# First block's output projections: order of updates, low parts and sums of squares around the norms, and the place of two weight loads in the queue

## The chip, the cores and the metric

The kernel runs on 1 core of one Trainium2 chip. The metric is the device time of one execution in microseconds (us). TensorE is called PE here, VectorE DVE, ScalarE ACT, and SyncE SP; SP issues the loads. Lines such as L901 are lines of the kernel before.

## What is computed

Two transformer blocks of two layers each run one after the other, on one sequence of 256 tokens with width 1024 (the first block adds 16 meta tokens, so it has 272 columns; its second layer drops them again at the output projection). Every layer of the first block ends its mixer with a projection `w_out` that is added to the residual, and then runs a gated feed-forward network (FFN) on the normed residual:

```
def rms_norm(x, g):
    xf = x.astype(jnp.float32)
    y = xf * lax.rsqrt(jnp.mean(xf * xf, axis=-1, keepdims=True) + EPS)
    return (y * g.astype(jnp.float32)).astype(x.dtype)
```

The second block is modulated by vectors `c @ w_ada + b_ada`. They depend on no token, so the kernel computes them in small pieces ("slots", 48 of them) scattered over the first block and the second.

## The kernel before, in words

The residual `H_t` lies transposed, eight tiles of 128 features by 272 (or 256) tokens. A product in float32 is made of three faster ones: an operand is split into a high part (rounded, by ACT) and a low part (the rest, by DVE), and PE adds high by high, high by low and low by high (line L901; 24 matmuls per output tile for 8 tiles of features).

Weights come in chunks of 1 MB into `raw`, a ring of RAW = 4 buffers. SP issues the loads in one fixed order (`load`, L782, for weights, and `ada_load`, L769, for slots), and each waits until the buffer's former chunk is done with: `sp.wait_ge(raw_done[...])`. A weight chunk is done when the low parts of both its halves are made (`split_lo`, L1535, from `raw` and the high part that `split_hi`, L2255, wrote); a slot chunk is done when PE has used it (`ada_sums`, L842).

The high and low parts go to `WH_t` and `WL_t`, four places each. `Linear.freed` tells which later half chunk may be split once an output tile is finished; with `w_out`, whose rest has four output tiles (k = 4 to 7), those are the two halves of the first two chunks of the next weights, `w_gu`.

`w_out` is two `Linear` objects: `first` (k = 0 to 3) and `rest` (k = 4 to 7). For each output tile PE writes a bank of `PA`; DVE adds it to the residual (L1597); ACT squares the new residual tile (`square`, L2291); DVE adds the square to the running sum `acc` (`accumulate`, L1546). The three engines each work through one queue in order, and this order is written out by hand in `linear_dve` and `linear_act`:

```
elif L.stat and k >= (KD - 3 if L.kt == KD else KD - 1):
    accumulate(L.stat, k)
    deferred.extend(todo[q])
elif L.stat:
    splits(q)
    accumulate(L.stat, k)
```

So for k = 0 to 4 of `w_out` DVE makes the freed low part between the residual's update and the accumulation, and for k = 5, 6 and 7 it puts the low part off (`deferred`) until after the norm's reciprocal. ACT makes the high part ahead of its wait for the residual's update, for all k but 7.

Then the norm (class `Norm`; `norm_pe`, `norm_dve`, `norm_act`). PE multiplies `acc` by ones, four matmuls of a quarter of the tokens each, which gives the sums over features in four groups of partitions (L1043; the trace shows each as two passes); ACT takes the root (L2491), DVE the reciprocal (L1701), PE spreads it over all partitions (L1056), ACT copies it to `rt` (L2501), and DVE scales the residual with it (L1716), tile by tile; ACT rounds the high part (L2513) and DVE makes the low part (L1724). The first linear after it, `w_gu`, goes over the tiles as they come: `four_tiles` computes four output tiles at a time, first with the weights' high parts (L961), last with the low parts (L989).

A norm can have slots of the modulation to fill PE's waits (`Norm.fill`, `norm_slots_pe`). In the two FFN norms of the first block there is one slot ahead of the sums ("start") and one behind the spreading ("end"). Their chunks are loaded ahead of all chunks of `w_gu`, because `tail_ada = AdaSlots(2)` stands ahead of the FFN in the plan.

There are six norms of this kind: the first (on the input), the two FFN norms of the first block, its second mixing norm, the norm that starts the second block, and the last one, behind the last FFN. The four others of the second block are of another class, `Joint`.

## Time and profile before

| what | value |
|---|---|
| median of 3 runs | 1711.11 us (1710.5 to 1714.62) |
| the profiled execution's own time | 1713.17 us |
| its span | 1711.2 us |
| PE busy | 1619.1 us, 95% of the span |
| DVE busy, ACT busy | 1020.6 us (60%), 869.0 us (51%) |
| mean granted TensorE clock | 0.979 |
| DMA | 253.92 MB, 148 GB/s |

A timeline row has the start, the duration, the engine, the line, the operation with output and inputs, how many in a row, and in brackets how long the engine stood idle before it and what it waited for. Durations of PE are of pipelined matmuls, so that starts overlap ends. The granted clock is 1.00 at 2.4 GHz and 0.50 at 1.2 GHz.

### The profile page before, as it was taken

To read this page: it belongs to the slowest core of one execution; us is meant where nothing else is said; L and a number is where in the kernel's file an instruction comes from. 1 tells how busy PE (TensorE), PEld (TensorE's weight loads), DVE (VectorE), ACT (ScalarE), POOL (GpSimd) and SP (SyncE) were. 2 spreads that over 40 slices of the span, in tenths; PEclk is the share of its full clock that TensorE was granted. 3 is DMA by queue.
4 is the path that set the end of the run, shared out by engine and by line. 5 is a ranking of instruction groups with operands and counts; after the bars stand their busy time and mean duration, and the time that the engine had idled before them with its cause. 6 is when DMAs were issued, how large, how long until landed. Compare 5 with 4: busy or idle time off the path is not lost.

```text
span 1711.2 us, 27924 instructions
## 1 busy us (share of the span) xinstructions
PE 1619.1 (95%) x11722; PEld 1419.0 (83%) x11722; DVE 1020.6 (60%) x1586; ACT 869.0 (51%) x1467; POOL 21.0 (1%) x38
## 2 busy tenths in 40 slices
PE   6998999989998999999989999999999898999997
PEld 6967999989778999887757778888888674789997
DVE  7665545465846555733464765425556777687676
ACT  6754434447545444535365544323444547666563
POOL 0000000000000000130000000000000000000000
PEclk9998999999998999999999999999999899999999
DMA  7364546354555464682201453232213530154642
GB/s 294 145 239 162 187 144 211 130 192 151 204 197 197 144 229 144 209 236 74 91 9 50 150 220 118 75 138 101 83 57 119 197 123 26 70 211 153 220 145 90
DMA packets 60523, 253.92 MB, mean 148 GB/s; under 512 B 4976, under 2 KB 8304, under 8 KB 42480
## 3 DMA queue, kind: packets, MB, share of 16 engines
q1 hardware_dynamic: 59088, 249.01, 40.0%
q0 software_dynamic: 1312, 3.15, 1.0%
q8 instruction: 93, 1.52, 0.3%
q14 instruction: 30, 0.25, 0.0%
HBM read 251.09 MB, written 1.05 MB: 147 GB/s over the span
## 4 chain that ended last, share of the span: by engine, by line
PE 62%; DVE 4%; ACT 3%; issue 1%; DVEq 0%; ACTq 0%
PE PA L901 49%; PE PA L961 3%; PE PB L1305 2%; PE PA L989 1%; PE PB L842 1%; PE PB L1292 1%; DVE WL_t L1535 1%; ACT tmp L2694 1%; PE PA L1377 1%; PE PA L937 1%; PE PA L938 1%; PE PA L943 1%; PE PA L1489 1%; PE PA L1383 0%; DVE small L2117 0%
## 5 line engine op out<-in xcount | busy, mean ns | idle before, releaser
L1535 DVE TENSOR_TENSOR WL_t<-raw,WH_t 128x1024 fp32r<-128x1024 f32 (+1 forms) x344 | 444.4, 1297 | 325.7 <-ACT WH_t L2255 325.4
L901 PE MATMUL PA<-XH_t,WH_t 128*128 128x256 f32 (+2 forms) x1984 | 630.2, 318 | 4.9 <-DVE XL_t L1724 2.3
L901 PE MATMUL PA<-XL_t,WH_t 128*128 128x256 f32 (+2 forms) x1984 | 624.8, 315 | 0.0
L901 PE MATMUL PA<-XH_t,WL_t 128*128 128x256 f32 (+2 forms) x1984 | 624.7, 315 | 0.0
L2255 ACT ACTIVATE WH_t<-raw 128x1024 fp32r<-128x1024 f32 (+1 forms) x344 | 380.9, 1112 | 172.1 <-PE PA L901 143.2
L901 PEld LDWEIGHTS PA<-XH_t,WH_t 128*128 128x128 f32 x1984 | 377.2, 190 | 34.7 <-issue 7.9
L901 PEld LDWEIGHTS PA<-XL_t,WH_t 128*128 128x128 f32 x1984 | 377.3, 190 | 21.3 <-issue 0.5
L901 PEld LDWEIGHTS PA<-XH_t,WL_t 128*128 128x128 f32 x1984 | 377.2, 190 | 21.2
L901 PE MATMUL PA<-AH_t,WH_t 128*128 128x256 f32 (+2 forms) x616 | 192.2, 312 | 0.3 <-DVE AL_t L1581 0.2
L901 PE MATMUL PA<-AH_t,WL_t 128*128 128x256 f32 (+2 forms) x616 | 191.1, 310 | 0.0
L901 PE MATMUL PA<-AL_t,WH_t 128*128 128x256 f32 (+2 forms) x616 | 190.5, 309 | 0.0
L1651 DVE SCALAR_TENSOR_TENSOR tmp<-PA,par,tmp 128x510 f32<-128x510 f32 (+1 forms) x88 | 53.7, 614 | 121.8 <-ACT tmp L2409 121.8
L2409 ACT ACTIVATE tmp<-PA,par 128x512 f32<-128x512 f32 (+1 forms) x88 | 58.4, 667 | 133.7 <-PE PA L901 126.0
L901 PEld LDWEIGHTS PA<-AH_t,WL_t 128*128 128x128 f32 x616 | 115.8, 188 | 6.8
L901 PEld LDWEIGHTS PA<-AH_t,WH_t 128*128 128x128 f32 x616 | 115.8, 188 | 6.6 <-DVE AL_t L1581 0.9
L901 PEld LDWEIGHTS PA<-AL_t,WH_t 128*128 128x128 f32 x616 | 115.7, 188 | 6.4
L2366 ACT ACTIVATE big<-PA 128x272 f32<-128x272 f32 (+2 forms) x68 | 31.6, 465 | 122.4 <-PE PA L901 109.8
L961 PE MATMUL PA<-XH_t,WH_t 128*128 128x256 f32 (+1 forms) x288 | 52.4, 318 | 5.4 <-DVE XL_t L1724 2.7
L842 PE MATMUL PB<-raw,cpad_t 128*32 128x256 f32 x768 | 57.2, 422 | 0.0
L961 PEld LDWEIGHTS PA<-XH_t,WH_t 128*128 128x128 f32 x288 | 44.6, 218 | 13.9 <-issue 9.4
L2694 ACT ACTIVATE tmp<-PA,small 128x512 f32<-128x512 f32 (+1 forms) x64 | 40.2, 638 | 26.2 <-DVE small L2117 26.2
L2117 DVE TENSOR_REDUCE small<-PA 128x1 f32<-128x512 f32 (+1 forms) x64 | 36.8, 618 | 27.1 <-PE PA L1489 13.2
(277 smaller groups left out, 1705.2 us busy)
## 6 DMA issues: line engine op xcount, KB each, us to landing
raw<-in_w_ada SPq DMA_DIRECT2D x48, 1024.0 KB, 4.9
raw<-in_w_gu SPq DMA_DIRECT2D x44, 1024.0 KB, 4.8
raw<-in_w_dn SPq DMA_DIRECT2D x64, 704.0 KB, 4.0
raw<-in_w_up SPq DMA_DIRECT2D x44, 1024.0 KB, 4.8
raw<-in_w_in SPq DMA_DIRECT2D x30, 1024.0 KB, 4.9
raw<-in_w_out SPq DMA_DIRECT2D x12, 1024.0 KB, 4.8
raw<-in_w_qkv SPq DMA_DIRECT2D x6, 1024.0 KB, 6.6
raw<-in_w_outc SPq DMA_DIRECT2D x4, 1024.0 KB, 4.8
```

What stands on the lines that cost most here:

```text
L842: mm = pe.matmul(ada_psum[b // 6][0][32 * j:32 * j + 32, :], cpad[:, k, :], RAWV[:, r % RAW, c:c + 256], start=(k == 0), stop=(k == 7))
L901: mm = pe.matmul(PA[:, (L.b0 + o) % 4, 0:T], W[:, c:c + P], X[:, k, L.x0:L.x0 + T], start=(n == 0 and m == 0 and not L.early), stop=(n == ...
L937: pe.matmul(PA[:, bank, 0:L.T], WH_t[:, c:c + P], hi[:, k, 0:L.T], start=(k == 0), stop=False)
L961: pe.matmul(PA[:, bank % 4, a:b], WH_t[:, c:c + P], x[:, k, a:b], start=(k == 0 and x is hi), stop=False)
L1305: mm = pe.matmul(PB[64 * c:64 * c + 64, v % 2, 0:256], value(v, c, kb), a_PT(second, v % 2)[c][:, j, :], start=(j == 0), stop=(j == len(bl ...
L1535: dve.tensor_tensor(WL_t[:, w:w + L.cols], RAWV[:, r % RAW, part * UNIT:part * UNIT + L.cols], WHf[:, w:w + L.cols], ALU.subtract).then_in ...
L1651: dve.scalar_tensor_tensor(c[:, :, 1:SEQ], ps[:, :, 0:SEQ - 1], tap(o, 0), c[:, :, 1:SEQ], ALU.mult, ALU.add).then_inc(S("conv_left"), 1)
L2117: dve.tensor_reduce(a_m[p % 3][:, c:c + 1], PA[:, 2 * (p % 2) + c, 0:width(p)], AX_X, ALU.max, negate=True).then_inc(S(name + "_m"), 1)
L2255: act.activation(WH_t[:, w:w + L.cols], RAWV[:, r % RAW, part * UNIT:part * UNIT + L.cols], ACT.Copy).then_inc(S("w_hi"), 1)
L2366: act.activation(L.dst[:, k, 0:T], PA[:, (L.b0 + o) % 4, 0:T], ACT.Copy).then_inc(S("of_act"), 1)
L2409: act.activation(conv[s % 2][x][:, 0:T], PA[:, (L.b0 + o) % 4, 0:T], ACT.Identity, bias=biasv(L.layer)[:, bass.ds(c, 1)], scale=tapv(L.lay ...
L2694: act.activation(a_P[p % 3][c][:, 0:w], PA[:, 2 * (p % 2) + c, 0:w], ACT.Exp, bias=a_m[p % 3][:, c:c + 1], accum_out=a_s[p % 3][:, c:c + 1 ...
```

## The change

- `Norm` gets a number `own`: 3 for a norm behind `w_out` (kt == KD), 1 for a norm behind an FFN, 0 for the first. The squares of the last `own` tiles are written to places of their own in `tmp` (`own_squares`), DVE does not accumulate them, and PE adds them itself: four matmuls for `acc`, then four for each own square, in one accumulation.
- Behind `w_out`, DVE accumulates the square of tile k - 1 after the update of tile k, and makes the low part that tile k - 1 freed after that; only the last low part is put off past the reciprocal. ACT waits for the update and squares first, and makes the freed high part after that.
- In the two FFN norms the slot "start" becomes a slot "amid", between the sums and the spreading. Both slots' chunks are now loaded behind the first two chunks of `w_gu` (`held=2`).

```diff
-            def __init__(self, kind, l, T, src, groups, alone=False):
+            def __init__(self, kind, l, T, src, groups, alone=False, own=0):
...
-                self.a0 = take("n_acc", KD - 1)
+
+                self.own = own
+                self.a0 = take("n_acc", KD - 1 - own)
...
-            n = Norm(*a, alone=not writers)
+            n = Norm(*a, alone=not writers, own=0 if not writers else 3 if writers[-1].kt == KD else 1)
...
-            tail_ada = AdaSlots(2)
             n = norm([first, rest], "pre", l, T, HV, [(0, T, ("ffng", l), None)])
-            n.fill(tail_ada.slots(), start=1, end=1)
-            writers = [ffn(l, T, "glu", w_gu1, w_dn1, HV, tiles_ready(n), mods=(0, 0, 6) if l else None)[1]]
+
+
+            up, last = ffn(l, T, "glu", w_gu1, w_dn1, HV, tiles_ready(n), held=2, mods=(0, 0, 6) if l else None)
+            n.fill(up.slots(), amid=1, end=1)
+            writers = [last]
...
+        def own_squares(n, k):
+
+
+            return tmp[:, 1536 + (KD - 1 - k) * 512:1536 + (KD - 1 - k) * 512 + n.T]
...
-                pe.wait_ge(S("n_acc"), n.value("n_acc", KD - 1))
+                pe.wait_ge(S("n_acc"), n.value("n_acc", KD - 1 - n.own))
...
-                for j in range(4):
-                    x = acc[:, j * w:(j + 1) * w] if n.T < T2 else quarter(acc, j)
-                    o = PB[32 * j:32 * j + 32, 0, 0:w]
-                    mm = pe.matmul(o if n.T < T2 else o.rearrange("p (h t) -> p h t", h=2), ones[:, 0:32], x,
-                                   start=True, stop=True)
+                for k in range(KD - 1 - n.own, KD):
+                    x = acc if k == KD - 1 - n.own else own_squares(n, k)
+                    if x is not acc:
+
+                        pe.wait_ge(S("n_sq"), n.value("n_sq", k))
+                    for j in range(4):
+                        q = x[:, j * w:(j + 1) * w] if n.T < T2 else quarter(x, j)
+                        o = PB[32 * j:32 * j + 32, 0, 0:w]
+                        mm = pe.matmul(o if n.T < T2 else o.rearrange("p (h t) -> p h t", h=2), ones[:, 0:32], q,
+                                       start=x is acc, stop=k == KD - 1)
                 mm.then_inc(S("n_sum"), 1)
+                norm_slots_pe(n, "amid")
...
-                if k == 0:
+                if k == 0 or k >= KD - n.own:
                     return
...
-                            elif L.stat and k >= (KD - 3 if L.kt == KD else KD - 1):
-                                accumulate(L.stat, k)
-                                deferred.extend(todo[q])
-                            elif L.stat:
+                            elif L.stat and L.kt == FH and k < KD - 1:
                                 splits(q)
                                 accumulate(L.stat, k)
+                            elif L.stat:
+
+                                if L.kt == KD:
+                                    accumulate(L.stat, max(k - 1, 0))
+                                for x in late:
+                                    split_lo(*x)
+                                late[:] = todo[q]
+                                if k == KD - 1:
+                                    deferred.extend(late)
+                                    late.clear()
...
+                elif k >= KD - n.own:
+                    dst = own_squares(n, k)
...
-                                last = k == KD - 1
-                                if not last:
+                                ahead = L.kt == FH and k < KD - 1
+                                if ahead:
                                     splits(q)
...
-                                if last:
+                                if k == KD - 1:
                                     deferred.extend(todo[q])
+                                elif not ahead:
+                                    splits(q)
```

How the rows move is shown at the first FFN norm (first layer of the first block). Each row has the line, the operation and how often it stands in a row.

DVE before, from the update of tile k = 4 on. `H_t<-H_t,PA` is an update, `WL_t<-raw,WH_t` a low part of weights, `tmp<-tmp` an accumulation:

```order
L1597 TENSOR_TENSOR H_t<-H_t,PA 128x272
L1535 TENSOR_TENSOR WL_t<-raw,WH_t 128x1024
L1546 TENSOR_TENSOR tmp<-tmp 128x272
L1597 TENSOR_TENSOR H_t<-H_t,PA 128x272
L1546 TENSOR_TENSOR tmp<-tmp 128x272
L1597 TENSOR_TENSOR H_t<-H_t,PA 128x272
L1546 TENSOR_TENSOR tmp<-tmp 128x272
L1597 TENSOR_TENSOR H_t<-H_t,PA 128x272
L1546 TENSOR_TENSOR tmp<-tmp 128x272
L1701 RECIPROCAL tmp<-tmp 128x68
L1535 TENSOR_TENSOR WL_t<-raw,WH_t 128x1024
```
DVE in the change, from the update of tile k = 4 on:

```order
L1612 TENSOR_TENSOR H_t<-H_t,PA 128x272
L1561 TENSOR_TENSOR tmp<-tmp 128x272
L1550 TENSOR_TENSOR WL_t<-raw,WH_t 128x1024
L1612 TENSOR_TENSOR H_t<-H_t,PA 128x272
L1561 TENSOR_TENSOR tmp<-tmp 128x272
L1550 TENSOR_TENSOR WL_t<-raw,WH_t 128x1024
L1612 TENSOR_TENSOR H_t<-H_t,PA 128x272
L1550 TENSOR_TENSOR WL_t<-raw,WH_t 128x1024
L1612 TENSOR_TENSOR H_t<-H_t,PA 128x272
L1550 TENSOR_TENSOR WL_t<-raw,WH_t 128x1024
L1723 RECIPROCAL tmp<-tmp 128x68
L1550 TENSOR_TENSOR WL_t<-raw,WH_t 128x1024
```
No low part stands between an update and the accumulation of its own tile any longer, three accumulations are gone, and two low parts more stand ahead of the reciprocal, each behind a later tile's update; one stands behind it, as before.

PE before: the last matmuls of `w_out`, a slot, the sums, the spreading, a slot, the first of `w_gu`:

```order
L901 MATMUL PA<-XL_t,WH_t 128x272
L901 MATMUL PA<-XH_t,WL_t 128x272
L842 MATMUL PB<-raw,cpad_t 32x256 x8
L1043 MATMUL PB<-tmp,cboth 32x68 x4
L1056 MATMUL PA<-tmp,spread 128x68 x4
L842 MATMUL PB<-raw,cpad_t 32x256 x8
L961 MATMUL PA<-XH_t,WH_t 128x272 x4
```
PE in the change, the same place:

```order
L910 MATMUL PA<-XL_t,WH_t 128x272
L910 MATMUL PA<-XH_t,WL_t 128x272
L1057 MATMUL PB<-tmp,cboth 32x68 x16
L851 MATMUL PB<-raw,cpad_t 32x256 x8
L1071 MATMUL PA<-tmp,spread 128x68 x4
L851 MATMUL PB<-raw,cpad_t 32x256 x8
L970 MATMUL PA<-XH_t,WH_t 128x272 x4
```
The sums grow from 4 to 16 matmuls and stand directly behind `w_out`; the slot that stood ahead of them stands behind them.

SP before, the loads from `w_out`'s first half on:

```order
L782 DMA raw<-in_w_out 128x2048 x2
L769 DMA raw<-in_w_ada 128x4x512 x8
L782 DMA raw<-in_w_out 128x2048 x2
L769 DMA raw<-in_w_ada 128x4x512 x4
L782 DMA raw<-in_w_gu 128x2048 x11
L782 DMA raw<-in_w_dn 128x1408 x8
```
SP in the change:

```order
L791 DMA raw<-in_w_out 128x2048 x2
L778 DMA raw<-in_w_ada 128x4x512 x8
L791 DMA raw<-in_w_out 128x2048 x2
L778 DMA raw<-in_w_ada 128x4x512 x2
L791 DMA raw<-in_w_gu 128x2048 x2
L778 DMA raw<-in_w_ada 128x4x512 x2
L791 DMA raw<-in_w_gu 128x2048 x9
```
Two chunks of `w_gu` have moved ahead of the last two slots' chunks (the first two of the four after `w_out` belong to the mixer and stay).

## Rows read from the trace of the kernel before

**Rows 1.** The page, part 4: the chain that ended last, by engine.

```profile
PE 62%; DVE 4%; ACT 3%; issue 1%; DVEq 0%; ACTq 0%
```

**Rows 2.** DVE timeline, first FFN norm (start us, us, engine line op, [idle before <-releaser]).

```profile
148.91 0.43 DVE L1597 TENSOR_TENSOR H_t<-H_t,PA 128x272 f32<-128x272 f32 x1
157.23 1.23 DVE L1535 TENSOR_TENSOR WL_t<-raw,WH_t 128x1024 fp32r<-128x1024 f32 x1 [7.89 <-ACT WH_t L2255]
...
161.29 0.43 DVE L1597 TENSOR_TENSOR H_t<-H_t,PA 128x272 f32<-128x272 f32 x1
162.27 0.44 DVE L1546 TENSOR_TENSOR tmp<-tmp 128x272 f32<-128x272 f32 x1 [0.55 <-ACT tmp L2291]
163.64 0.58 DVE L1701 RECIPROCAL tmp<-tmp 128x68 f32<-128x68 f32 x1 [0.93 <-ACT tmp L2491]
...
165.48 0.92 DVE L1716 SCALAR_TENSOR_TENSOR tmp<-H_t,par,tmp 128x272 f32<-128x272 f32 x2 [0.19 <-ACT tmp L2501]
```

**Rows 3.** ACT timeline, the same stretch.

```profile
156.14 1.06 ACT L2255 ACTIVATE WH_t<-raw 128x1024 fp32r<-128x1024 f32 x1 [8.16 <-DMA raw<-in_w_gu]
...
161.81 0.43 ACT L2291 ACTIVATE tmp<-H_t 128x272 f32<-128x272 f32 x1 [0.90 <-DVE H_t L1597]
163.29 0.32 ACT L2491 ACTIVATE tmp<-PB,small 128x68 f32<-128x68 f32 x1 [1.05 <-PE PB L1043]
```

**Rows 4.** PE timeline, the same stretch.

```profile
157.37 0.29 PE L901 MATMUL PA<-XH_t,WL_t 128*128 128x272 f32 x1
157.59 1.07 PE L842 MATMUL PB<-raw,cpad_t 128*32 128x256 f32 x16
162.76 0.45 PE L1043 MATMUL PB<-tmp,cboth 128*32 128x68 f32 x8 [4.11 <-DVE tmp L1546]
...
164.27 0.71 PE L1056 MATMUL PA<-tmp,spread 32*128 32x68 f32 x8 [1.05 <-DVE tmp L1701]
...
167.17 1.25 PE L961 MATMUL PA<-XH_t,WH_t 128*128 128x272 f32 x4 [0.33 <-DVE XL_t L1724]
...
171.63 0.67 PE L961 MATMUL PA<-XL_t,WH_t 128*128 128x272 f32 x4
```

**Rows 5.** SP queue: two issues; then two DMA issues, KB, us to landing.

```profile
145.00 0.37 SPq L769 DMA_DIRECT2D raw<-in_w_ada  x1
...
148.67 0.37 SPq L769 DMA_DIRECT2D raw<-in_w_ada  x1
...
raw<-in_w_ada SPq DMA_DIRECT2D x1, 1024.0 KB, 4.9
...
raw<-in_w_gu SPq DMA_DIRECT2D x1, 1024.0 KB, 7.0
```

**Rows 6.** Second FFN norm: ACT timeline, then PE timeline.

```profile
511.35 1.06 ACT L2255 ACTIVATE WH_t<-raw 128x1024 fp32r<-128x1024 f32 x1 [8.53 <-DMA raw<-in_w_gu]
...
518.35 0.31 ACT L2491 ACTIVATE tmp<-PB,small 128x64 f32<-128x64 f32 x1 [1.02 <-PE PB L1043]
...
517.83 0.44 PE L1043 MATMUL PB<-tmp,cboth 128*32 128x64 f32 x8 [5.21 <-DVE tmp L1546]
```

**Rows 7.** Stretches, line L961 alone: window, PE busy, PEld busy, granted clock.

```profile
167.10:177.20 10.10, 10.03 (x64) 10.00 (x64) 0.79 0.72 272
522.10:531.90 9.80, 9.75 (x64) 9.57 (x64) 0.78 0.74 288
```

**Rows 8.** Stretches of 1 us on PE at the first FFN norm.

```profile
161.00:162.00 1.00, 0.00 (x0) 0.55 0.98 418
```

**Rows 9.** Second mixing norm: PE timeline, then its clock in 1 us.

```profile
371.63 0.33 PE L1043 MATMUL PB<-tmp,cboth 128*32 128x68 f32 x8 [1.51 <-DVE tmp L1546]
...
372.00:373.00 1.00, 0.00 (x0) 0.87 0.06 12
```

**Rows 10.** DVE timeline: last accumulation before second block, and at the end.

```profile
714.99 0.69 DVE L1546 TENSOR_TENSOR tmp<-tmp 128x512 f32<-128x512 f32 x1 [0.74 <-ACT tmp L2291]
...
1699.81 0.42 DVE L1546 TENSOR_TENSOR tmp<-tmp 128x256 f32<-128x256 f32 x1 [0.53 <-ACT tmp L2291]
```

More of the change, by code:

```diff
@@ L1569, in tail_product @@
                                   ALU.mult).then_inc(S("j_b"), 1)
-            deferred = []
+            deferred, late = [], []
             def linear_dve(L):
```

## The prediction

> **What bounds the kernel now.** I read the page's chain first: PE carries 62% of what ended last, and DVE and ACT come in short pieces [rows 1]. Time is to be had only where PE waits. So I went to the norms that the diff touches and read, for each, the timelines of PE, DVE and ACT, then the loads, then the granted clock.
>
> At the first FFN norm PE ends `w_out` at 157.66 (157.37 + 0.29), does the "start" slot, and then stands idle for 4.11 us until the last accumulation [rows 4]. DVE shows why. The update of tile 4 starts at 148.91; the low part queued behind it waits 7.89 us for ACT's high part, and the updates of tiles 5 to 7, whose matmuls PE had done long before or by then, come only after it, the last at 161.29 [rows 2]. ACT's high part waited 8.16 us for the load of the first chunk of `w_gu` [rows 3]. That load is late because it stands behind two slot chunks in SP's queue: the second slot's load was issued at 148.67, the first `w_gu` chunk came right behind it and took 7.0 us to land, where a load with nothing ahead takes 4.9 [rows 5]. The second FFN norm repeats it: a wait of 8.53 us for `w_gu`, and PE idle for 5.21 us [rows 6]. So a load that nobody needs for another 10 us holds up, through two in-order queues, a sum that everybody waits for.
>
> The idle time has a second price. The granted clock stays at 1.00 while PE is busy and falls inside the idle gap (0.55 on average in the microsecond from 161) [rows 8]. The first 64 matmuls of `w_gu` (L961) then run at a mean clock of 0.79 and 0.78 and take 10.03 and 9.75 us [rows 7]; a group of four takes 1.25 us in the slow part (some 0.91 from start to start) and 0.67 (0.51 from start to start) once the clock is back [rows 4].
>
> **The change, part by part.** DVE's updates of tiles 5 to 7 stand ahead of their low parts, and ACT's squares ahead of its high parts. Behind `w_out`'s end at 157.66 the path is then: update at 157.70; square 0.52 later, as 161.29 and 161.81 are apart, at 158.22 [rows 2, 3]; where the accumulation stood (0.46 after the square's start) PE now starts the last four sums itself, at about 158.7; with 0.33 us for a sum at full clock [rows 9] the root starts at 159.1 instead of 163.29 [rows 3]: **4.2 us less**. At the second FFN norm `w_out` ends at 511.6 (the sums start at 517.83 after 5.21 idle, and the slot ahead took 1.0) and the same 1.4 us give a root at 513.05 instead of 518.35 [rows 6]: **5.3 us less**.
>
> This needs the loads to keep up. DVE makes each low part of `w_out` one tile later, which moves the buffer releases: the first `w_gu` load goes out some 1.1 us after the place at which the first slot load went (145.00), at 146.1 [rows 5], and the second some 1.9 us after 148.67, behind an update and an accumulation, at about 150.6. With 4.9 us they land by 151.5 and 155.5. ACT has to have made the third high part (1.06 us [rows 3]) before 158.2, so the second chunk may land at 157.1: 1.6 us to spare, at the second FFN norm about 0.9. The low parts of `w_out`'s own tiles stay ahead of PE by about 1.5 us. Both are cover that I cost at nothing; a load later than that costs one for one.
>
> The sums: 12 matmuls more behind `w_out`, 24 passes. Eight passes take at most 0.33 us at full clock [rows 9], so 24 take at most 1.0; `acc` and squares 5 and 6 are ready at 157.66, and PE has 1.05 us before the last square. Nothing. Three accumulations less on DVE (0.44 each [rows 2]) count above only through the last.
>
> The slot "amid" takes 1.07 us at full clock, and 1.05 us pass between sums and spreading [rows 4]. It fits, if its chunk has landed: behind the second `w_gu` chunk, about 158.0 (155.5 plus 2.5: the first `w_gu` chunk landed at 156.1 and the slot ahead of it at 153.6 [rows 5]), needed at 158.9. At the second norm that is 512.7 against 512.8, and I take 0.3 us for waits there. Bounds: nothing to 1 us at each. SP's queue holds the same loads; only the order of the four changes, at 0.37 us an issue.
>
> Behind the reciprocal DVE makes the one deferred low part. Its high part is made only after the root now, where before it was long there: the root's 0.32, 1.06 for the high and 1.23 for the low part put the scaling up to 0.4 us later in the chain than 165.48 has it [rows 2, 3]. Taken: 0.24 at each, 0.5 together.
>
> The clock. PE's longest gap at these norms shrinks from 4.11 and 5.21 us to about 1.3 us, and two slots of 1.0 us stand in it. If the clock stays up, L961 takes 16 groups of 0.51 us and 0.48 us, with 0.2 of waits for the first tiles 8.3 and 7.9 us instead of 10.03 and 9.75: **3.6 us less** for both. The rows at the second mixing norm warn: there PE's longest gap was only 1.51 us, and the clock fell all the same (0.87 in the microsecond from 372) [rows 9]. But there PE did next to nothing else in some 6 us, while here two slots come. I take the clock as staying up.
> The Trainium skill ("TensorE: Matmul & The Clock Gate", "Why this matters for your kernels") asks only that there be no long idle gaps between bursts of matmuls; by that rule the clock would stay up here, and also at the second mixing norm, where the trace disagrees with it.
>
> Three norms behind an FFN lose only the last accumulation from the path: 0.44 at the second mixing norm (as rows 2), 0.69 at the start of the second block and 0.42 at the end [rows 10]. The first two are followed by a stretch at the lower clock whose end need not move with them. Taken: 0.4, 0.6 and 0.5 with the hand-over, **1.5 us**.
>
> Sum: 4.2 + 5.3 + 3.6 + 1.5 - 0.5 - 0.3 = 13.8 us. The profiled execution's span of 1711.2 becomes 1697.4, and its own time of 1713.17 becomes 1699.4; that execution was 2 us above the median of 1711.11, so the median becomes **1697.3**. Behind `w_gu`'s start PE is the engine that is waited for, so nothing later should eat the gain.
>
> **Rivals.**
> 1. The clock falls anyway, in the new, shorter gap. For it: the second mixing norm [rows 9]. Against: two slots of real matmuls in the gap. Then 3.6 us are not won, and the slot "amid" may run at half speed and hold the spreading by 0.9 at one norm: 9.3 to 10.2 us, about 1701. Chance 0.22.
> 2. The loads are late by a few microseconds: `w_gu`'s second chunk lands after 157.1 (the longest landing here, 7.0 us, would be 157.6), or the slot's chunk lands late and PE, in order, holds the spreading for it. 1.5 to 4 us at each norm, and the clock with them: a gain of 5 to 8 us, about 1704. Chance 0.12.
> 3. The new order is slower, through the slot "amid". Before, no slot stood between the sums and the spreading; now PE stops there for a chunk that is queued behind two others, and the spreading, the scaling and all of `w_gu` are queued behind it. Each microsecond of landing past 158.9 costs one. To eat 13.8 us at two norms the chunk must be 7 us late at each, that is land 15 us after its issue at about 151. The rows have 4.9 alone and 7.0 second in the queue, and I reckon with 7. Chance 0.02, time 1713 to 1718.
> 4. The change does less than it says: something else (the copies, the weights' low parts) sets the start of `w_gu`, and only the accumulations are won, 0.5 us at each of five norms. Against: both waits end in `w_gu`'s landing. 1708 to 1709. Chance 0.04.
>
> **How the numbers follow.** My forecast has 0.60. Its own range is 13.8 plus or minus 2 (the slots' waits up to 1.7 us more, the clock's edges at the other norms, which move by up to a microsecond each way), 1695 to 1699.5. The range that should hold the time 8 times in 10 goes up over rival 1 and part of rival 2: 1694.5 to 1703.5. About 0.3%, or 5.1 us, is what a measurement can tell from no change, so faster means below 1706: the forecast, rival 1, nearly all of rival 2 and some of rival 4, 0.93; the same 0.05; slower 0.02.
>
> **What would show it.** In the profile after, at the first FFN norm: DVE's updates of tiles 5 to 7 start 0.04 us behind PE's tiles, with no wait of 8 us anywhere on DVE; ACT waits for `w_gu` once, for 2 us or so, behind the square of tile 4; the sums show 32 passes, the last eight some 1.0 us after `w_out`'s end; the spreading starts 1.0 us behind the root; L961 starts about 5.4 us after `w_out`'s end (before 9.5) and takes 8.3 us at clock 1.00. I am wrong if DVE or ACT still stands for a load ahead of the square of tile 7, if PE waits for a slot's load ahead of the spreading, or if the clock falls before L961.

## The result and the profile after

The change takes 1702.45 us (median of 6 runs, 1701.05 to 1707.42), the kernel before on the same chip 1711.25 (6 runs, 1710.38 to 1718.37). The ratio is 0.9947, with a 95% interval of 0.9933 to 0.996: 8.8 us less, in the range, where 13.8 were forecast. The profiled execution of after is the slowest of its six: own time 1707.42, span 1705.6. So its total says little; its stretches say much.

Read first what the page's chain says, and how far back it reaches. The shares of after sum to the whole span. Those of before [rows 1] sum to 70%: its chain is followed back from the end only to 516.03 us, and its first FFN norm is not on it. So 62% and 83% for PE can't be compared. What the chain of after does show is that one load of `w_ada`, the slots' weights, is on it: it starts at 501.81 and takes 10.70 us, at the second FFN norm.

```profile
PE 83%; DVE 9%; ACT 6%; issue 2%; DMA 1%; SPq 0%; DVEq 0%; ACTq 0%
```

**First FFN norm.** DVE's timeline of after (start us, us, engine line op, [idle before <-releaser]; L1612 is the update, L1550 the low part, L1723 the reciprocal, L1738 the scaling), to hold against [rows 2]:

```profile
155.74 0.44 DVE L1612 TENSOR_TENSOR H_t<-H_t,PA 128x272 f32<-128x272 f32 x1 [1.08 <-PE PA L910]
156.09 1.22 DVE L1550 TENSOR_TENSOR WL_t<-raw,WH_t 128x1024 fp32r<-128x1024 f32 x1
158.75 0.44 DVE L1612 TENSOR_TENSOR H_t<-H_t,PA 128x272 f32<-128x272 f32 x1 [1.44 <-PE PA L910]
...
160.51 0.58 DVE L1723 RECIPROCAL tmp<-tmp 128x68 f32<-128x68 f32 x1 [0.18 <-ACT tmp L2517]
161.46 1.23 DVE L1550 TENSOR_TENSOR WL_t<-raw,WH_t 128x1024 fp32r<-128x1024 f32 x1 [0.37 <-ACT WH_t L2277]
162.60 0.91 DVE L1738 SCALAR_TENSOR_TENSOR tmp<-H_t,par,tmp 128x272 f32<-128x272 f32 x2
```

ACT's timeline, to hold against [rows 3] (L2277 high part, L2315 square, L2517 root):

```profile
152.10 1.06 ACT L2277 ACTIVATE WH_t<-raw 128x1024 fp32r<-128x1024 f32 x1 [1.42 <-DMA raw<-in_w_gu]
...
159.28 0.43 ACT L2315 ACTIVATE tmp<-H_t 128x272 f32<-128x272 f32 x1 [1.63 <-DVE H_t L1612]
160.16 0.32 ACT L2517 ACTIVATE tmp<-PB,small 128x68 f32<-128x68 f32 x1 [0.45 <-PE PB L1057]
```

And PE's timeline, to hold against [rows 4] (L910 the products of `w_out`, L1057 the sums, L851 a slot, L1071 the spreading, L970 and L998 those of `w_gu` with its high and its low parts):

```profile
158.43 0.29 PE L910 MATMUL PA<-XH_t,WL_t 128*128 128x272 f32 x1
158.65 0.56 PE L1057 MATMUL PB<-tmp,cboth 128*32 128x68 f32 x24
159.77 0.33 PE L1057 MATMUL PB<-tmp,cboth 128*32 128x68 f32 x8 [0.56 <-ACT tmp L2315]
159.91 1.05 PE L851 MATMUL PB<-raw,cpad_t 128*32 128x256 f32 x16
161.14 0.45 PE L1071 MATMUL PA<-tmp,spread 32*128 32x68 f32 x8 [0.19 <-DVE tmp L1723]
162.02 1.07 PE L851 MATMUL PB<-raw,cpad_t 128*32 128x256 f32 x16 [0.42 <-DMA raw<-in_w_ada]
164.28 0.74 PE L970 MATMUL PA<-XH_t,WH_t 128*128 128x272 f32 x4 [1.20 <-DVE XL_t L1746]
...
172.40 0.79 PE L998 MATMUL PA<-XH_t,WL_t 128*128 128x272 f32 x5
```

The wait of 7.89 us on DVE is gone, ACT waits 1.42 us for `w_gu`, and PE's 4.11 us have shrunk to 0.56 for the last square. `w_out` ends at 158.72 (158.43 + 0.29); the root follows 1.44 us behind (160.16), where before it took 5.63. L970 starts 5.56 us behind `w_out`'s end and takes 8.12 us to L998's start, at full clock. (L998's row counts 5 because the stretch shown ends there.) So the first product with a low part of `w_gu` (L998) stands 13.68 us behind `w_out`'s end; before it stood 19.55 behind. I use this distance as the measure of a norm from here on, since it holds the waits and the clock together: **5.9 us won** at this norm.

**Second FFN norm.** PE's timeline of after, to hold against [rows 6]:

```profile
507.44 0.32 PE L1057 MATMUL PB<-tmp,cboth 128*32 128x64 f32 x8 [0.55 <-ACT tmp L2315]
509.87 1.26 PE L851 MATMUL PB<-raw,cpad_t 128*32 128x256 f32 x16 [2.12 <-DMA raw<-in_w_ada]
511.07 0.70 PE L1071 MATMUL PA<-tmp,spread 32*128 32x64 f32 x8
512.55 1.93 PE L851 MATMUL PB<-raw,cpad_t 128*32 128x256 f32 x16 [0.79 <-DMA raw<-in_w_ada]
514.42 1.22 PE L970 MATMUL PA<-XH_t,WH_t 128*128 128x256 f32 x4
...
523.51 0.76 PE L998 MATMUL PA<-XH_t,WL_t 128*128 128x256 f32 x5
```

`w_out` ends at 506.41 and the root is again 1.41 us behind it. Then PE stands 2.12 us for the chunk of the slot "amid", with the spreading queued behind. The chunk's load went out 6.14 us ahead of `w_out`'s end and took 9.6 us. The chunk of the slot "end" is late too: PE stands 0.79 us more for it, the slot takes 1.93 us, and L970 follows it with no idle time. This is the load that the chain names. Issues of DMA of after, in the stretch 500.2 to 500.4 (KB, us to landing):

```profile
raw<-in_w_ada SPq DMA_DIRECT2D x1, 1024.0 KB, 9.6
```

Then the clock falls. Stretches of 1 us of after (window, length, busy time of PE, PEld, DVE, ACT, POOL, then granted clock, DMA share, GB/s); the first is the first FFN norm, where before had 0.55 [rows 8]:

```profile
161.00:162.00 1.00, 0.45 (x8) 0.31 (x8) 0.63 (x2) 0.76 (x2) 0.00 (x0) 1.00 1.11 444
...
510.00:511.00 1.00, 1.00 (x16) 0.29 (x12) 0.34 (x1) 0.00 (x0) 0.00 (x0) 0.81 0.97 403
511.00:512.00 1.00, 0.77 (x12) 0.52 (x8) 0.00 (x0) 0.16 (x1) 0.00 (x0) 0.50 1.07 436
```

The stretches of L970 alone (PE busy, PEld busy, clock), to hold against [rows 7]:

```profile
164.10:172.60 8.50, 8.28 (x64) 8.08 (x64) 1.00 0.88 359
514.30:523.60 9.30, 9.18 (x64) 9.05 (x64) 0.83 0.64 250
```

The low parts start 17.10 us behind `w_out`'s end, before 20.11: **3.0 us won** where I had 6.9.

**The other norms.** At the second mixing norm the root is 1.44 us behind the end of the products, before 1.91; at the start of the second block 1.81, before 2.52. The clock falls at the mixing norm as before [rows 9], and at the start of the second block in both. Not all of the 0.71 us is kept there: the first product with a low part comes 15.84 us behind the end of the products in after and 17.07 in a second trace of the same kernel (k8_after_again below), before 16.71. Over the nine traces in which PE adds the last square at this norm the mean is 16.40, over the four without 16.97.

**What this execution lost elsewhere.** Two losses don't belong to the norms. It reached `w_out`'s end at the first FFN norm 1.06 us later than before did, though nearly all of the program up to there is the same; the 192 matmuls of `w_out` take 31.59 us with no idle time, before 31.60, so the loss lies ahead of them. And in the attention of the second block PE stands while ACT makes exponentials, and the clock falls there, in a stretch that had 1.00 in the trace of before (1400 to 1420). PE's timeline, then 1 us of clock of after:

```profile
1409.21 2.08 PE L1504 MATMUL PA<-big 64*128 64x512 f32 x4 [2.75 <-ACT tmp L2720]
```

```profile
1408.00:1409.00 1.00, 0.00 (x0) 0.00 (x0) 0.22 (x1) 1.00 (x5) 0.00 (x0) 0.66 1.04 391
```

### The profile page after: what moved, and what is told of

It reads as the page before. It is cut to its first block, busy times and chain, and to the rows that moved or that the text cites. A ratio compares the mean times of both kernels' runs of the same rounds, so it can differ in the third digit from the quotient of the medians.

```text
span 1705.6 us, 28040 instructions
## 1 busy us (share of the span) xinstructions
PE 1619.8 (95%) x11794; PEld 1418.1 (83%) x11794; DVE 1017.1 (60%) x1577; ACT 869.4 (51%) x1467; POOL 21.1 (1%) x38
## 4 chain that ended last, share of the span: by engine, by line
PE 83%; DVE 9%; ACT 6%; issue 2%; DMA 1%; SPq 0%; DVEq 0%; ACTq 0%
PE PA L910 63%; PE PA L970 4%; DVE WL_t L1550 2%; PE PB L851 2%; PE PB L1320 2%; PE PA L998 2%; PE PB L1307 1%; ACT WH_t L2277 1%; PE PA L946 1%; PE PA L947 1%; PE PA L952 1%; PE PA L865 1%; PE PA L1504 1%; PE PB L1250 1%; DMA raw<-in_w_ada 1%
## 5 line engine op out<-in xcount | busy, mean ns | idle before, releaser
L910 PE MATMUL PA<-XH_t,WH_t 128*128 128x256 f32 (+2 forms) x1984 | 629.6, 317 | 4.9 <-DVE XL_t L1746 2.4
L1550 DVE TENSOR_TENSOR WL_t<-raw,WH_t 128x1024 fp32r<-128x1024 f32 (+1 forms) x344 | 444.5, 1297 | 312.0 <-ACT WH_t L2277 311.6
L910 PE MATMUL PA<-XL_t,WH_t 128*128 128x256 f32 (+2 forms) x1984 | 624.1, 315 | 0.0
L910 PE MATMUL PA<-XH_t,WL_t 128*128 128x256 f32 (+2 forms) x1984 | 623.8, 314 | 0.0
L2277 ACT ACTIVATE WH_t<-raw 128x1024 fp32r<-128x1024 f32 (+1 forms) x344 | 380.8, 1111 | 155.2 <-PE PA L910 139.7
L910 PEld LDWEIGHTS PA<-XH_t,WH_t 128*128 128x128 f32 x1984 | 376.8, 190 | 34.5 <-issue 7.9
L910 PEld LDWEIGHTS PA<-XH_t,WL_t 128*128 128x128 f32 x1984 | 376.9, 190 | 21.6
L910 PEld LDWEIGHTS PA<-XL_t,WH_t 128*128 128x128 f32 x1984 | 377.2, 190 | 21.2 <-issue 0.5
L910 PE MATMUL PA<-AH_t,WH_t 128*128 128x256 f32 (+2 forms) x616 | 192.0, 312 | 0.3 <-DVE AL_t L1596 0.2
L910 PE MATMUL PA<-AH_t,WL_t 128*128 128x256 f32 (+2 forms) x616 | 190.9, 310 | 0.0
L910 PE MATMUL PA<-AL_t,WH_t 128*128 128x256 f32 (+2 forms) x616 | 190.3, 309 | 0.0
L910 PEld LDWEIGHTS PA<-AH_t,WL_t 128*128 128x128 f32 x616 | 115.6, 188 | 6.8
L910 PEld LDWEIGHTS PA<-AH_t,WH_t 128*128 128x128 f32 x616 | 115.6, 188 | 6.6 <-DVE AL_t L1596 0.9
L910 PEld LDWEIGHTS PA<-AL_t,WH_t 128*128 128x128 f32 x616 | 115.6, 188 | 6.5
L2390 ACT ACTIVATE big<-PA 128x272 f32<-128x272 f32 (+2 forms) x68 | 31.6, 465 | 123.2 <-PE PA L910 110.1
L851 PE MATMUL PB<-raw,cpad_t 128*32 128x256 f32 x768 | 55.6, 413 | 3.3 <-DMA raw<-in_w_ada 3.3
L970 PE MATMUL PA<-XH_t,WH_t 128*128 128x256 f32 (+1 forms) x288 | 50.0, 306 | 7.4 <-DVE XL_t L1746 3.5
L970 PEld LDWEIGHTS PA<-XH_t,WH_t 128*128 128x128 f32 x288 | 42.2, 206 | 14.7 <-issue 10.0
```

The source lines that it names most:

```text
L851: mm = pe.matmul(ada_psum[b // 6][0][32 * j:32 * j + 32, :], cpad[:, k, :], RAWV[:, r % RAW, c:c + 256], start=(k == 0), stop=(k == 7))
L910: mm = pe.matmul(PA[:, (L.b0 + o) % 4, 0:T], W[:, c:c + P], X[:, k, L.x0:L.x0 + T], start=(n == 0 and m == 0 and not L.early), stop=(n == ...
L970: pe.matmul(PA[:, bank % 4, a:b], WH_t[:, c:c + P], x[:, k, a:b], start=(k == 0 and x is hi), stop=False)
L1550: dve.tensor_tensor(WL_t[:, w:w + L.cols], RAWV[:, r % RAW, part * UNIT:part * UNIT + L.cols], WHf[:, w:w + L.cols], ALU.subtract).then_in ...
L2277: act.activation(WH_t[:, w:w + L.cols], RAWV[:, r % RAW, part * UNIT:part * UNIT + L.cols], ACT.Copy).then_inc(S("w_hi"), 1)
L2390: act.activation(L.dst[:, k, 0:T], PA[:, (L.b0 + o) % 4, 0:T], ACT.Copy).then_inc(S("of_act"), 1)
```

## The experiments

What they had to decide. The theory of the **loads**: the gain is all in their place (third part of the change: no slot chunk ahead of `w_gu`), and the new order on DVE and ACT makes the slot's chunk late, because it moves the release of the buffers. Its rival, the **order**: the updates and squares ahead of the splits are what frees the sum. And for the loss at the second norm a rival of its own: it is the **clock** that fell there by itself, and not the late chunk. Below, "1st" and "2nd" are the distance from `w_out`'s end to the first product with a low part of `w_gu`, in the profiled execution; before has 19.55 and 20.11, the change 13.68 and 17.10.

**k1_old_slots: the change with the loads in their old place.**

```diff
+            tail_ada = AdaSlots(2)
             n = norm([first, rest], "pre", l, T, HV, [(0, T, ("ffng", l), None)])
-            up, last = ffn(..., held=2, ...)
-            n.fill(up.slots(), amid=1, end=1)
+            n.fill(tail_ada.slots(), start=1, end=1)
+            writers = [ffn(...)[1]]
```

> The change without its third part: updates ahead of low and high parts and own squares as in the change, but both slots' chunks are loaded ahead of w_gu again, and the slots stand at start and end. Theory (the place of the loads is what frees the sum): w_gu's first chunk lands some 0.3 us before w_out's end or later, at both FFN norms ACT stands for it with the squares of tiles 5 to 7 queued behind, the root comes at most 1 us earlier than before, and the gain is that of the three norms behind an FFN, 1.5 us, plus 0.5: about 1709.5. Rival (the order of updates and low parts is what frees it): as the whole change, about 1702.5.

Measured: 1714.02 us (12 runs), before 1713.11 (18 runs): ratio 1.0013 (1.0001 to 1.0024). 1st 19.79, 2nd 20.64. The new order and the three squares alone win nothing at the FFN norms, as ACT's timeline at the first one shows:

```profile
159.24 1.06 ACT L2275 ACTIVATE WH_t<-raw 128x1024 fp32r<-128x1024 f32 x1 [8.33 <-DMA raw<-in_w_gu]
160.20 0.41 ACT L2313 ACTIVATE tmp<-H_t 128x272 f32<-128x272 f32 x1
```

The same 8 us as [rows 3], one tile later: a square is now ahead of the high part of its own tile, but still behind that of the tile before. The first chunk of `w_gu` lands 0.28 and 1.69 us behind `w_out`'s end, where before it landed 1.60 and 0.35 ahead of it. The order moves a wait and takes none away. The time missed its forecast of 1709.5: the roots at the three other norms came 0.4 to 0.7 us earlier, and yet the kernel is no faster than before. The section on the prediction comes back to this.

**k2_slots_alone and k11_slots_again: before with the third part alone.** The old order on DVE and ACT, and all eight accumulations on DVE.

```diff
                 mm.then_inc(S("n_sum"), 1)
+                norm_slots_pe(n, "amid")
...
-            n.fill(tail_ada.slots(), start=1, end=1)
+            up, last = ffn(..., held=2, ...)
+            n.fill(up.slots(), amid=1, end=1)
```

> The kernel before with the third part of the change alone: slots amid and end, their chunks behind the first two of w_gu; the order on DVE and ACT and the sums are those of before. Theory: w_gu's first chunk goes out at the place of the first slot's load and lands 6 us before w_out's end, so updates and squares no longer wait; the root comes 0.45 us later than in the change (the last accumulation is on the path), but the loads go out 1 to 2 us earlier than in the change, so that PE does not wait for the slot amid at the second FFN norm and the clock stays up there: 12 us less than before, about 1699, at least as fast as the whole change. Rival (all three parts are needed): 1704 to 1708, with DVE's low parts still ahead of updates.

> k2_slots_alone again. Theory: as the change or 1 us below it, 9 to 10 us below the kernel before; PE never waits for the slot amid.

Measured: 1702.93 (5 runs), before 1713.11, ratio 0.995 (0.9936 to 0.9964); again, on another chip, 1704.01 (6 runs), before 1711.7, ratio 0.995 (0.9935 to 0.9964). This one part has the ratio of the whole change; the 1699 that I expected at first was too low. 1st 13.64, 2nd 13.14 (again 13.64 and 13.15). PE's timeline at the first FFN norm of k2_slots_alone, and the last sums and the slots of the second:

```profile
157.53 0.33 PE L1045 MATMUL PB<-tmp,cboth 128*32 128x68 f32 x8 [1.52 <-DVE tmp L1549]
157.68 1.05 PE L844 MATMUL PB<-raw,cpad_t 128*32 128x256 f32 x16
...
505.12 0.32 PE L1045 MATMUL PB<-tmp,cboth 128*32 128x64 f32 x8 [1.47 <-DVE tmp L1549]
505.26 1.05 PE L844 MATMUL PB<-raw,cpad_t 128*32 128x256 f32 x16
...
506.84 1.07 PE L844 MATMUL PB<-raw,cpad_t 128*32 128x256 f32 x16
```

No slot waits at either norm. The slot "amid" has its chunk 0.52 us ahead of `w_out`'s end at the second. Only the accumulation is left, 1.52 and 1.47 us of idle PE, and the clock stays up over it. The theory of the order falls, that of the loads stands.

**k3_early_low: the change, but tiles 0 to 3 of `w_out` in the old order.**

```diff
-                            elif L.stat and L.kt == FH and k < KD - 1:
+                            elif L.stat and k < (KD - 1 if L.kt == FH else KD // 2):
```

(and the same bound for ACT's squares and for the accumulation one tile back)

> The change, but for tiles 0 to 3 of w_out DVE and ACT make the freed parts as early as in the kernel before; the new order holds from tile 4 on. Theory (what is missing from the forecast is PE's wait of 2.1 us for the slot amid at the second FFN norm, and the clock that falls in it): the second w_gu chunk and both slots' chunks go out some 1.5 us earlier, PE's wait for the slot at the second FFN norm shrinks below 0.6 us, the clock stays at 1.00 there, and the time is 2.5 to 3.5 us below the change, about 1699.5. Rival (what is missing is the clock's phase in the second block's attention, which differs from execution to execution): as the change, 1702.5.

Measured: 1701.24 (5 runs), ratio 0.9936 (0.9922 to 0.9951). 1st 15.25, 2nd 13.23. The time lies between what theory and rival gave, and its interval overlaps the change's. At the second norm the slot's load goes out 7.71 us ahead of `w_out`'s end, not 6.14, and the slot "amid" doesn't wait. At the first norm nothing on PE waits for a load, and the clock falls all the same. PE's timeline there (the second row is cut off by the end of its stretch), then stretches of 1 us:

```profile
156.98 1.07 PE L851 MATMUL PB<-raw,cpad_t 128*32 128x256 f32 x16
159.74 0.57 PE L970 MATMUL PA<-XH_t,WH_t 128*128 128x272 f32 x2 [1.69 <-DVE XL_t L1746]
```

```profile
159.00:160.00 1.00, 0.26 (x2) 0.29 (x3) 0.96 (x3) 0.49 (x3) 0.00 (x0) 1.00 0.97 197
160.00:161.00 1.00, 1.00 (x6) 1.00 (x6) 1.00 (x4) 0.78 (x2) 0.00 (x0) 0.50 0.86 344
```

1.6 us at this norm are the clock's alone (15.25 against 13.68). So rival 1 of the prediction is real without any late load.

**k4_no_own1: the change, but squares summed by PE only behind `w_out`.** (`own=3` there, 0 at the norms behind an FFN.)

> The change without own squares behind an FFN (own = 3 behind w_out, 0 elsewhere). Theory: the last accumulation is on the path at three norms again, 0.44, 0.69 and 0.42 us, so the time is 1.0 to 1.5 us above the change, about 1704. Rival (the clock's edges do not move with the work, so the two norms followed by a stretch at the lower clock give nothing): 0.5 us above the change.

Measured: 1706.58 (7 runs), ratio 0.9962 (0.9947 to 0.9978). The roots of the other norms are back at 1.91 and 2.52 us. By the traces that is 1.6 us over the three norms (0.47, 0.71 and 0.46); the difference from the ratio of the change, 0.9962 to 0.9945 (k8_after_again), would be 2.9, with intervals that overlap. 1st 13.67, 2nd 16.58, and again PE waits for the slot "amid":

```profile
511.80 1.07 PE L851 MATMUL PB<-raw,cpad_t 128*32 128x256 f32 x16 [1.14 <-DMA raw<-in_w_ada]
```

**k8_after_again: the change once more, on another chip.**

> The change again, on the chip of the next three, to compare them with. Theory: at the second FFN norm PE again waits 1 to 2.5 us for the slot amid, since its chunk lands 1 us or more behind the sums, and w_gu's low parts start 16.5 to 17.5 us behind w_out's end (13.7 at the first norm). Rival (that wait was one execution's accident): below 14.5 us at both.

Measured: 1704.09 (5 runs), before 1713.37 (9 runs), ratio 0.9945 (0.993 to 0.9959). 1st 13.68, 2nd 14.55: 5.6 us won where the first trace had 3.0. The 14.55 is outside the 16.5 to 17.5 of the theory and just above the rival's bound of 14.5, so the size of the first trace's loss was in large part that one execution's. PE's timeline at the second FFN norm:

```profile
505.74 1.07 PE L851 MATMUL PB<-raw,cpad_t 128*32 128x256 f32 x16 [0.20 <-DMA raw<-in_w_ada]
506.74 0.45 PE L1071 MATMUL PA<-tmp,spread 32*128 32x64 f32 x8
508.43 1.79 PE L851 MATMUL PB<-raw,cpad_t 128*32 128x256 f32 x16 [1.24 <-DMA raw<-in_w_ada]
510.15 1.23 PE L970 MATMUL PA<-XH_t,WH_t 128*128 128x256 f32 x4
```

A wait of 0.20 us, then one of 1.24 that in part overlaps what DVE needs anyway, and the second slot at 1.79 us instead of 1.07, since the clock had fallen. The size of the loss differs from one execution to the next; its place doesn't.

**k5_end2 and k6_early_end2: no slot between sums and spreading.** k5 is the change with both slots behind the spreading, k6 is k3_early_low with the same.

```diff
-            n.fill(up.slots(), amid=1, end=1)
+            n.fill(up.slots(), end=2)
```

> The change with both slots behind the spreading. Theory: at the second FFN norm the spreading starts 2.4 us behind w_out's end instead of 3.5 to 4.6, but the second slot's chunk lands at +5 to +6 and PE does it ahead of w_gu, so w_gu starts at +6 to +7 instead of +7 to +8: 1 us less there. At the first norm both slots end at +4.4 to +5.3, ahead of w_gu's start at +5.57: nothing. The time is 1 to 2 us below the change. Rival (with no matmuls between the sums and the spreading the clock falls at both norms): 1 to 3 us above the change.

> Early low parts for tiles 0 to 3, and both slots behind the spreading. Theory: the chunks are there in time in either place, so it is as with the slot amid (w_gu starts 5.5 us behind w_out's end at both norms): the time of k3_early_low, 1.2 us below the change. Rival on the clock: the slot amid keeps it up; without it the clock falls, and the low parts of w_gu start 15 to 16 us behind w_out's end at both norms: 2 to 3 us above k3_early_low.

Measured: k5 1702.26 (5 runs), ratio 0.9931 (0.9918 to 0.9943), 1st 13.67, 2nd 13.23; k6 1701.86 (5 runs), ratio 0.9931 (0.9919 to 0.9944), 1st 13.67, 2nd 13.95. In k5 the chunk still lands 1.42 us behind `w_out`'s end, but nobody needs it before 2.74, so the second norm gets its full 6.9 us. In k6 no slot waits for its chunk at all, and yet the clock falls at the second norm and takes 0.7 us. PE's timeline there, then 1 us:

```profile
505.94 0.45 PE L1071 MATMUL PA<-tmp,spread 32*128 32x64 f32 x8 [1.02 <-DVE tmp L1723]
...
507.00:508.00 1.00, 1.00 (x16) 0.52 (x12) 1.00 (x3) 0.07 (x1) 0.00 (x0) 0.61 0.80 336
```

The interval of k5 overlaps that of the change (0.993 to 0.9959): the traces put it 1.3 us (k8) to 3.9 us (after) ahead at the second norm, and the timings alone don't decide.

**k7_slots_own1 and k10_own1_again: the parts that were worth it.** The third part, the old order on DVE and ACT, and one square summed by PE at all five norms.

```diff
-own=0 if not writers else 3 if writers[-1].kt == KD else 1
+own=1 if writers else 0
...
-                            elif L.stat and L.kt == FH and k < KD - 1:
-                                splits(q)
-                                accumulate(L.stat, k)
-                            elif L.stat:
-                                ...
+                            elif L.stat and k >= (KD - 3 if L.kt == KD else KD - 1):
+                                accumulate(L.stat, k)
+                                deferred.extend(todo[q])
+                            elif L.stat:
+                                splits(q)
+                                accumulate(L.stat, k)
...
-                                ahead = L.kt == FH and k < KD - 1
+                                ahead = k < KD - 1
```

> The slots' third part with the old order on DVE and ACT, and one own square at all five norms: it beats both kernels if the order of low parts is worth nothing. Theory: as the slots alone, less 0.45 us at each FFN norm and 1.0 to 1.5 us at the three others; 2 us below k2_slots_alone and 1.5 us below the change. Rival (updates ahead of low parts matter): as k2_slots_alone, above the change.

> k7_slots_own1 again, beside the slots alone on the same chip. Theory: 2.3 us (0.45 at five norms, 0.7 for one of them) below k11_slots_again, and w_gu's low parts start 13.3 and 12.7 us behind w_out's end. Rival (its lead over the change came from where the clock fell in those executions): no lead over the slots alone.

Measured: 1696.44 (5 runs), before 1713.37, ratio 0.991 (0.9894 to 0.9926); again, on another chip, 1697.79 (6 runs), before 1711.7, ratio 0.992 (0.9905 to 0.9935). This beats both kernels: the first interval lies wholly below the change's. But the lead over the slots alone (k2, k11) is 6.5 and 6.2 us in the medians, where 2 and 2.3 were expected and the traces give 0.4 to 0.5 us at each norm. The rest is not shown to be the square's. From the end of the products ahead of the second block to the end of the last products, k7 and k10 take 982.7 us, k2 and k11 989.3 and 988.2; the clock falls at about 1400 and 1452 us in k2 and k11 and not in k7 and k10, and the programs differ there by that one norm alone. 1st 13.25, 2nd 12.69 (again 13.17 and 12.69). PE's timeline of k10_own1_again, first and second FFN norm:

```profile
159.06 0.33 PE L1057 MATMUL PB<-tmp,cboth 128*32 128x68 f32 x8 [0.79 <-ACT tmp L2308]
159.20 1.05 PE L851 MATMUL PB<-raw,cpad_t 128*32 128x256 f32 x16
160.44 0.45 PE L1071 MATMUL PA<-tmp,spread 32*128 32x68 f32 x8 [0.19 <-DVE tmp L1716]
160.82 1.07 PE L851 MATMUL PB<-raw,cpad_t 128*32 128x256 f32 x16
163.08 0.74 PE L970 MATMUL PA<-XH_t,WH_t 128*128 128x272 f32 x4 [1.19 <-DVE XL_t L1739]
...
509.07 1.07 PE L851 MATMUL PB<-raw,cpad_t 128*32 128x256 f32 x16 [0.65 <-DMA raw<-in_w_ada]
510.56 0.71 PE L970 MATMUL PA<-XH_t,WH_t 128*128 128x256 f32 x4 [0.41 <-DVE XL_t L1739]
```

Here `w_gu` starts 5.07 us behind `w_out`'s end (4.94 at the second), not 5.57 (5.48 in k5). DVE's timeline at the second norm tells why: its one deferred low part follows the reciprocal with no wait, since ACT made the high part long ago. At the first norm of after it waited 0.37 for ACT and started 0.95 us behind the reciprocal's start, here 0.47.

```profile
507.37 0.55 DVE L1716 RECIPROCAL tmp<-tmp 128x64 f32<-128x64 f32 x1 [1.30 <-ACT tmp L2510]
507.84 1.16 DVE L1550 TENSOR_TENSOR WL_t<-raw,WH_t 128x1024 fp32r<-128x1024 f32 x1
508.92 0.87 DVE L1731 SCALAR_TENSOR_TENSOR tmp<-H_t,par,tmp 128x256 f32<-128x256 f32 x2
```

**k9_own3_old_order: the same with the change's three squares behind `w_out`.** That is, the change without its new order and nothing else.

> The whole change except its new order on DVE and ACT: slots amid and end behind two chunks of w_gu, three own squares behind w_out, one behind an FFN; low and high parts where they stood before. Theory: the accumulations of tiles 5 and 6 are hidden anyway, so three own squares are worth what one is, and the time is that of k7_slots_own1 within 0.5 us, 3 to 7 us below the change. Rival (the order is worth something once the squares are PE's): above k7_slots_own1.

Measured: 1700.41 (6 runs), before 1711.7, ratio 0.993 (0.9917 to 0.9944). 1st 13.17, 2nd 12.69, to the hundredth those of k10_own1_again: with three squares or with one, the last square is what is waited for. Its clock fell in the trace at places far from these norms where that of k10 did not (at 1406 and 1454 us), so the 2.6 us between the medians of k9 and k10 are not shown to be the squares', and the intervals overlap.

**The slot's load, over all traces.** At the second FFN norm, in us from `w_out`'s end; the slot "amid" needs the chunk at +1.2 (+1.6 where DVE makes the last accumulation, +2.7 in k5 and k6):

| Order on DVE and ACT | issued | took | landed |
|---|---|---|---|
| new (after, k4, k8, k5) | -6.14 | 9.55, 8.57, 7.64, 7.56 | +3.41, +2.43, +1.50, +1.42 |
| old, or old for tiles 0 to 3 (k2, k11, k7, k10, k9, k6, k3) | -7.71 | 7.19, 7.09, 7.34, 7.09, 8.50, 8.55, 8.68 | -0.52, -0.62, -0.36, -0.61, +0.79, +0.85, +0.97 |

From issue to need the new order leaves 7.3 us, and all four loads took longer; the old one leaves 8.9, and all seven took less. That is the late chunk of the slot "amid", and no clock is needed for it. The rival of the clock holds in part: k3 (first norm) and k6 (second) show it falling with no wait of PE for any load.

## Why the prediction was right and wrong

- **"PE carries 62% of what ended last."** Misread: the chain of [rows 1] covers 70% of the span, from 516.03 us on, so this is 62 of 70. Nothing in the sum rests on it.
- **The root, 4.2 and 5.3 us.** Right: 1.44 and 1.41 us behind `w_out`'s end, against 5.63 and 6.73 before, so 4.2 and 5.3. But I gave the whole to the order on DVE and ACT. k1 shows that the order wins none of it, and k2 that the place of the loads wins all but 0.4 to 0.5, the last accumulation. The row that I had quoted, `w_gu` landing in 7.0 us behind two slots [rows 5], held the whole cause; with the loads in time, the order of the queue behind them doesn't matter.
- **"This needs the loads to keep up."** The issues were right: 11.48 and 7.04 us ahead of `w_out`'s end for `w_gu`, forecast 11.56 and 7.06 (first norm).
- **The slot "amid", "0.3 us for waits there".** This is the step that failed. At the first norm no wait, and 2.7 us from the chunk of `w_gu` to the slot's, forecast 2.5. At the second norm I had reckoned the chunk at 512.7 against a need at 512.8, that is with no cover, and with the same 2.5; measured 4.93, 4.12 and 2.92, and waits of 2.12, 1.14 and 0.20 us. My upper bound of 1 us was too low: [rows 5] has one landing of each kind, and I took its scatter to be nothing. The first step to see was that the new order moves the issue 1.57 us back for no gain.
- **The clock, "I take the clock as staying up", 3.6 us.** Right at the first norm: 1.00 throughout, 8.1 us for the 64 matmuls. Wrong at the second, in after, k4 and k8: 9.1 us in after. 2.12 us of wait for the slot "amid" became 3.9 us of loss (17.10 against the 13.23 of k5): the chunk of the slot "end" was late as well, and from 510.6 us on the clock was at its lower level. Rival 1 named this, rival 2 the late slot's chunk; both came, at one norm.
  The rule of the Trainium skill that I had weighed ("TensorE: Matmul & The Clock Gate", "Why this matters for your kernels": no long idle gaps between bursts) doesn't sort these cases by a gap's length. The clock fell at a longest gap of 1.69 us (k3, first norm), 1.24 us (k8, second norm) and 1.02 us (k6, second norm), and held at 1.52 (k2, first norm) and 1.20 (the first norm of after).
- **"Taken: 0.24 at each"** for the deferred low part: measured 0.49 and 0.54 (5.57 and 5.48 against 5.08 and 4.94 of k9).
- **The three other norms, 1.5 us.** Right within 0.2 for the roots: 0.47, 0.71 and, at the end, 0.46 (from the last square to the root 0.85 us, k4 1.32). At the start of the second block the low parts came on average 0.6 us earlier, but from trace to trace they move by more than that (15.84 to 17.07 us), as I had warned of the stretches at the lower clock.
- **The sum.** By the traces the FFN norms gave 5.9 and 3.0 to 5.6 us, the others 1.6: 10.5 to 13.1, where the forecast was 13.8. The medians give 8.8, with an interval of 6.8 to 11.5. So part of the gain at the norms does not reach the end; k2 and k11 likewise show 12.9 at their norms and 10.2 and 7.7 in the medians. I had written "nothing later should eat the gain". That failed. The median lies above the forecast's own 1695 to 1699.5 and inside the wider range only because that one went up over rivals 1 and 2, not because this was foreseen.
  By an estimate from every run's mean granted clock, what eats it is more time at the lower clock elsewhere. The traces of before and k1 have 10.2 us at the lower clock at each FFN norm, those of k2 and k11 none. If every run of before is like its trace in this, the mean clock should rise by 20.4 / 2 / 1711 = 0.006. It rose from 0.9819 (38 runs of before) to 0.9832 (11 runs of k2 and k11). So the time at the lower clock outside the two FFN norms went from some 41 us to some 57 (in the change 47, in k7 and k10 46, in k1 53), and each of these costs up to half its length. This is of the size of what is missing here and in k1. Why the falls move to other places stays open; in after one lies in the attention of the second block, which k8 and k9 show too, but k10 doesn't.

## What to carry to other kernels

When an in-order engine waits for a load that a later stage needs, look first at what stands ahead of that load in the DMA queue, and put the load needed last behind it; reordering the engines' work is worth trying only after that. Any reordering of work that releases buffers moves every load behind those buffers: write down, for each load, issue, longest landing seen, and need, and treat a cover under 2.5 us (the scatter of the landings here) as a likely wait. Test the parts of a change alone: here the place of the loads carried nearly all of the gain, and the new order cost some of it. And hold the gain at the stages against the gain in total: where they differ, something else has moved.

## What the runs showed of the hardware

- Ahead of the FFN norms a load of 1 MB takes 4.7 to 5.3 us with nothing ahead in nearly all traces (7.53 in k7 at the first norm). Issued 0.39 us behind another, a slot's load behind `w_gu` takes 7.2 to 7.3 us at the first FFN norm in ten of eleven traces (8.7 in k7), but 7.1 to 9.6 at the second. All seven traces there with three squares on PE have 7.56 or more, the four with one or none 7.1 to 7.3. I have no mechanism for that, and it stays open. What differs is how much of the load behind gets in: between issue and landing the core's queues moved 2.4 MB in k2 and k10 (7.19 and 7.09 us) but 3.0 MB in k9 (8.50) and 3.2 in after (9.55), at about one rate (336 to 351 GB/s). The chunk of `w_gu` ahead and the slot's own make at most 2.1 MB of it, so most of the rest was the next slot's.
- The same program (but for the order within `w_out`) reached `w_out`'s end at the first FFN norm between 154.2 us (k3) and 158.9 us (k1). The 192 matmuls of `w_out` take 31.6 us in every trace, so these 4.8 us come from ahead of the change, and single executions can't be compared by their spans, only by distances inside a stage.
